# Query-key products of the prompt attention with 64-row operands instead of zero-padded 128-row operands

## The reference, cut to what matters

```python
logits = jnp.einsum('bqhmd,bkhmd->bhmqk', q, k).astype(jnp.float32) * (DA_DH ** -0.5)   # m = 0, 1; d = 64
bias = jnp.transpose(rel_bias[t5_bucket(dist)].astype(jnp.float32), (2, 0, 1))
logits = jnp.where((dist >= 0)[None, None, None], logits + bias[None, :, None], -1e30)
p = jax.nn.softmax(logits, axis=-1)
attn = p[:, :, 0] - lam * p[:, :, 1]
return jnp.einsum('bhqk,bkhv->bqhv', attn, v.astype(jnp.float32))
```

## Time and profile before

| | us |
|---|---|
| median of 3 runs | 1989.22 |
| lowest and highest run | 1988.94, 1991.32 |
| span of the profiled execution | 1994.6 |
| prompt attention | from 480.3 to some 912 |
| TensorE busy in the whole span | 1665.6 |
| VectorE busy | 730.8 |
| ScalarE busy | 454.2 |
| GpSimd busy | 266.4 |

### The profile page before, as it was taken

One profiled execution on the slowest core, in us unless ns is written; L12 is line 12 of the kernel. 1 busy time (PEld: TensorE's weight loads), 2 busy tenths in 40 slices (PEclk: granted clock), 3 DMA queues, 4 the chain that ended last, 5 costly groups with the idle time before them and its releaser, 6 DMA issues. The chain is left out here.

```text
span 1994.6 us, 22007 instructions
## 1 busy us (share of the span) xinstructions
PE 1665.6 (84%) x7402; PEld 1105.3 (55%) x7403; DVE 730.8 (37%) x1498; ACT 454.2 (23%) x1062; POOL 266.4 (13%) x479
## 2 busy tenths in 40 slices
PE   6998989775999999886996999999799059999950
PEld 4565556553555566553444888888587024444420
DVE  4267767674353535351223211121322312212213
ACT  2233332331343333331223111010322001111100
POOL 1001010101222222212130000000000311111112
PEclk8999989886999989997997999999899579999975
DMA  7001200002010100006764411210412838666426
GB/s 211 0 1 55 64 12 11 1 23 82 12 55 1 53 3 23 1 23 199 245 213 138 146 32 33 63 32 1 131 64 85 224 90 309 245 235 250 175 86 218
DMA packets 140800, 191.83 MB, mean 96 GB/s; under 512 B 10375, under 2 KB 107646, under 8 KB 140702
## 3 DMA queue, kind: packets, MB, share of 16 engines
q1 hardware_dynamic: 125022, 137.48, 22.1%
q0 software_dynamic: 15680, 53.10, 7.6%
HBM read 151.86 MB, written 38.69 MB: 96 GB/s over the span
## 5 line engine op out<-in xcount | busy, mean ns | idle before, releaser
L940 PE MATMUL psum<-branch_part,kept 128*128 128x384 f32 (+1 forms) x576 | 202.4, 507 | 1.2 <-DVE branch_part L1170 1.2
L2127 PE MATMUL psum<-moe_part,kept 128*128 x416 | 186.9, 603 | 5.6 <-DVE kept L2195 3.3
L940 PEld LDWEIGHTS psum<-branch_part,kept 128*128 128x128 f32 (+1 forms) x576 | 109.0, 194 | 77.0 <-issue 19.4
L1604 PE MATMUL psum<-split 128*128 128x368 f32 x384 | 133.3, 347 | 0.0
L474 PE MATMUL psum<-kept,branch_part 128*128 128x368 f32 x384 | 124.9, 481 | 10.0 <-PEq L217 5.0
L1598 PE MATMUL psum<-kept,merge_part 128*128 128x368 f32 x384 | 125.6, 481 | 9.0 <-DMA merge_part<-w_da_out 9.0
L2127 PEld LDWEIGHTS psum<-moe_part,kept 128*128 128x128 f32 x416 | 78.4, 193 | 95.9 <-issue 95.9
L479 PE MATMUL psum<-branch_part,kept 128*128 128x512 f32 (+1 forms) x288 | 127.5, 597 | 1.3 <-DVE kept L660 1.3
L1605 PE MATMUL psum<-split 128*128 128x368 f32 x384 | 126.8, 330 | 0.0
L1606 PE MATMUL psum<-split 128*128 128x368 f32 x384 | 126.4, 329 | 0.0
L1653 DVE TENSOR_TENSOR merge_part<-merge_part,psum 128x368 f32<-128x368 f32 x48 | 23.6, 534 | 254.0 <-ACT merge_part L1629 254.0
(11 more groups left out here) (307 smaller groups left out, 2713.2 us busy)
## 6 DMA issues: line engine op xcount, KB each, us to landing
branch_part<-cache_k SPq DMA_DIRECT2D x64, 256.0 KB, 4.9
branch_part<-cache_v POOLq DMA_DIRECT2D x64, 256.0 KB, 5.0
moe_part<-w_gate SPq DMA_DIRECT2D x16, 1024.0 KB
moe_part<-w_up SPq DMA_DIRECT2D x16, 1024.0 KB
moe_part<-w_down SPq DMA_DIRECT2D x16, 1024.0 KB
expert_out<-kept POOLq DMA_DIRECT2D x26, 512.0 KB, 4.1
branch_part<-w_in SPq DMA_DIRECT2D x8, 1024.0 KB, 8.8
merge_part<-w_in SPq DMA_DIRECT2D x16, 512.0 KB
```

What stands on the lines that cost most here:

```text
L940: mm = pe.matmul(bank_of(("z", h, i))[:ROWS[i], 0:384], K["xT"][:, k, cols(i)], Wb[h % 2][:, k, :], start=(k == 0), stop=(k == KC - 1))
L1604: pe.matmul(banks[j], wh[c % 2][:, k, ch], xh[:, k, chunk(n)], start=(k == 0), stop=False)
L2127: mm = pe.matmul(psum[:, 2 + par, :], XT[par][:, k, :], K["GU"][:, bass.ds(KC * b + k, 1), :], start=(k == 0), stop=(k == KC - 1))
```

## The change

The zero-padded tensors qz are replaced by one tensor qT that holds both maps, and each query-key product takes the 64 rows of its map from qT and from kT. The products of the two maps follow each other chunk by chunk (map 0 and map 1 of keys 0 to 511, then of the next chunk, then of the 16 meta keys), and not all of map 0 and then all of map 1. In tile 8 of a head the semaphore `logits` is raised after the last chunk of map 1 and no more after that of map 0. The 16 extra columns of tile 8 (job e) go to the same bank for both maps, and map 1's product now waits for map 0's through a new semaphore, `first_meta`. ScalarE places queries with one copy and not two, and for tile 0 of a head writes Qs itself with two more. GpSimd no longer clears qz and no longer copies into Qs. The tensor `vecs` shares memory with the probabilities. The rest of the kernel is as it was.

```diff
-            slot += [("L", s, 0), ("L", s, 1)] + ([("e", s, 0)] if s % NQ == NQ - 1 else [])
+            slot += [("L", s, 0)] + ([("e", s, 0)] if s % NQ == NQ - 1 else [])
...
-        qz = [sb(2, TOK) for _ in range(2)]
+        qT = [sb(TOK) for _ in range(2)]
...
-            def scores(s, m):
+            def scores(s):
+
                 h, i = s // NQ, s % NQ
                 r = P if i else META
-                q = qz[h % 2][:, m, COL[i]:COL[i] + r]
-                if m == 0:
-                    pe.wait_ge(x_done, NT * h + i + 1)
-                    if s:
-                        pe.wait_ge(exp_done, 2 * s)
+                half = [slice(0, 64), slice(64, P)]
+                pe.wait_ge(x_done, NT * h + i + 1)
+                if s:
+                    pe.wait_ge(exp_done, 2 * s)
                 n = P * i
-                for c in range(0, n, 512):
-                    w = min(512, n - c)
-                    mm = pe.matmul(lg[m][:r, c:c + w], q, kT[h % 2][:, FIRST + c:FIRST + c + w], start=True, stop=True)
-                if n < SEQ:
-                    mm = pe.matmul(lg[m][:r, n:n + META], q, kT[h % 2][:, 0:META], start=True, stop=True)
-                    mm.then_inc(logits, 1)
-                elif m == 0:
-                    mm.then_inc(logits, 1)
+                chunks = [(c, min(512, n - c), FIRST + c) for c in range(0, n, 512)] + [(n, META, 0)] * (n < SEQ)
+                for c, w, k0 in chunks:
+                    for m in range(2):
+                        mm = pe.matmul(lg[m][:r, c:c + w], qT[h % 2][half[m], COL[i]:COL[i] + r], kT[h % 2][half[m], k0:k0 + w], start=True, stop=True)
+                        if c == chunks[-1][0] and (n < SEQ or m == 1):
+                            mm.then_inc(logits, 1)
...
                 for m in range(2):
-                    mm = pe.matmul(bank_of(("e", s, 0))[:, META * m:META * m + META], qz[h % 2][:, m, cols(i)],
-                                   kT[h % 2][:, 0:META], start=True, stop=True)
-                mm.then_inc(logits, 1)
+                    rows = slice(64 * m, 64 * m + 64)
+                    if m:
+                        pe.wait_ge(first_meta, h + 1)
+                    mm = pe.matmul(bank_of(("e", s, 0))[:, META * m:META * m + META], qT[h % 2][rows, cols(i)],
+                                   kT[h % 2][rows, 0:META], start=True, stop=True)
+                    mm.then_inc(logits if m else first_meta, 1)
...
-                for m in range(2):
-                    rows = slice(64 * m, 64 * m + 64)
-                    act.activation(qz[h % 2][rows, m, cols(i)], bank[rows, 0:r], ACT.Copy, scale=K["vecT"][rows, 18:19])
+                act.activation(qT[h % 2][:, cols(i)], bank[:, 0:r], ACT.Copy, scale=K["vecT"][:, 18:19])
+                if i == 0:
+                    if h == 0:
+                        act.wait_ge(setup, 1)
+                    for m in range(2):
+                        rows = slice(64 * m, 64 * m + 64)
+                        act.activation(K["Qs"][rows, DB * h:DB * h + DB, 16 * h + 8 * m:16 * h + 8 * m + 8],
+                                       bank[rows, META:FIRST].rearrange("p (b s) -> p b s", s=DS), ACT.Copy, scale=K["vecT"][rows, 18:19])
...
-            for h in range(2):
-                pool.memset(qz[h].rearrange("p a b -> p (a b)"), 0.0).then_inc(setup, 1)
             pool.memset(K["Qs"].rearrange("p a b -> p (a b)"), 0.0).then_inc(setup, 1)
-            pool.wait_ge(setup, 3)
+            pool.wait_ge(setup, 1)
```

More of the change, by code:

```diff
@@ L850, in phase_attention @@
             "logits", "max_done", "exp_done", "a_done", "a_turned", "a_act", "a_dve", "o_done", "ssq_done", "orstd_done", "og_done", "og_turned", "ob_done"))
-        kv_out = [sem("kv_out0"), sem("kv_out1")]
+        kv_out, first_meta = [sem("kv_out0"), sem("kv_out1")], sem("first_meta")
         Wb = [sb(KC, 384) for _ in range(2)]
-        qz = [sb(2, TOK) for _ in range(2)]
+        qT = [sb(TOK) for _ in range(2)]
         kT = [sb(TOK) for _ in range(2)]
@@ L859, in phase_attention @@
         Bn = [sb(256) for _ in range(HEADS)]
-        rel, rel31, relh, bucket, vecs = sb(HEADS), sb(HEADS), sb(HEADS, P), sb(ND), sb(HEADS, ND)
+        rel, rel31, relh, bucket = sb(HEADS), sb(HEADS), sb(HEADS, P), sb(ND)
         Pm = sb(2, SEQ + META)
+        vecs = Pm.rearrange("p a b -> p (a b)")[:, 0:HEADS * ND].rearrange("p (a b) -> p a b", b=ND)
         Am, aT = sb(SEQ + META), sb(NT, P)
@@ L1012, in _ @@
                 pe.matmul(psum[:, h, 0:ND], relh[0:33, h, :], bucket[0:33], start=True, stop=True).then_inc(bias_made, 1)
-            run = {"z": product, "x": turn_qk, "L": scores, "e": lambda s, _: meta_scores(s), "a": turn_probabilities,
+            run = {"z": product, "x": turn_qk, "L": lambda s, _: scores(s), "e": lambda s, _: meta_scores(s), "a": turn_probabilities,
                    "o": lambda s, _: outputs(s), "g": lambda s, _: turn_output(s)}
@@ L1041, in place_qk @@
                 act.wait_ge(x_turned, n + 1)
-                if n == 0:
-                    act.wait_ge(setup, 3)
                 if i == 0 and h >= 2:
                     act.wait_ge(saved, h - 1)
-                for m in range(2):
-                    rows = slice(64 * m, 64 * m + 64)
-                    act.activation(qz[h % 2][rows, m, cols(i)], bank[rows, 0:r], ACT.Copy, scale=K["vecT"][rows, 18:19])
+                act.activation(qT[h % 2][:, cols(i)], bank[:, 0:r], ACT.Copy, scale=K["vecT"][:, 18:19])
[6 more added lines that the diff above has]
+                                       bank[rows, META:FIRST].rearrange("p (b s) -> p b s", s=DS), ACT.Copy, scale=K["vecT"][rows, 18:19])
                 act.activation(kT[h % 2][:, cols(i)], bank[:, P:P + r], ACT.Copy).then_inc(x_done, 1)
@@ L1136, in save @@
                 pool.wait_ge(x_done, NT * h + 1)
-                for m in range(2):
-                    pool.tensor_copy(K["Qs"][:, DB * h:DB * h + DB, 16 * h + 8 * m:16 * h + 8 * m + 8],
-                                     qz[h % 2][:, m, META:FIRST].rearrange("p (b s) -> p b s", s=DS))
                 pool.tensor_copy(K["kS"][:, h, :], kT[h % 2][:, 0:FIRST]).then_inc(saved, 1)
```

## The result

The changed kernel takes 2013.65 us (median of 4 runs, 2007.51 to 2018.51), the kernel before 1989.41 beside it. The ratio is 1.0118, with a 95% interval of 1.0081 to 1.0155: slower by some 24 us, where 3.5 were forecast, and outside the range of 1984 to 2002. The profiled execution has a span of 2011.9 us, 17.3 more than the one of before. Each run's time on record is its span and 1.9 us, so the profiled execution of before (span 1994.6) stands for a time of some 1996.5, 7 us above its median and not 5.4. That is why the two profiles differ by less than the medians do.

A forecast was written before the change was run, and what follows sets the result against it. The prediction took the chain through VectorE to bound the block: start -2.6, chain +1.0, clock +2.7 and +2.4 sum to +3.5 us, which on 1989.2 gives 1992.7 us. The range was 1984 to 2002.

The forecast's parts named there:

- What bounds the block: Prompt attention: each slot lasts as long as the chain through VectorE, and TensorE's saved time lengthens its own wait.
- Two row halves at work together: Query-key products: the two maps overlap on the row halves, so about 61 us of streaming become 31 us.
- Rival 1: Query-key products: no overlap on the row halves, map 0 ends later, about +32 us, 2021 us; chance 0.12.
- rival 2: Query-key products: both matmuls of map 0's 32-bit product precede map 1's, which lags; 4.4 us in all, 1997; chance 0.25.
- The terms of the chain: Slots of the prompt attention: shape changes +3.6 and +0.3 us, less waiting for map 1 and e -2.9, sum +1.0.
- The start: Start of the block: VectorE's table copy no longer held up by GpSimd's clearing, all behind it earlier, -2.6 us.
- The clock: TensorE falls to half clock after stretches with little work: +2.7 us and +2.4 us.
- the fourth head to lose its luck: Gap between heads, where the clock had held once: expected to fall there too, +3.3 x 0.8 = +2.7 us.
- one more such stretch and a little in the last slots: Short tiles: one more stretch at half clock, like head 0's loss of 1.7 us, and a little more, +2.4 us.

The follow-up runs named there:

- e2: Kernel before, its zero-padded 128-row products kept, but map 0 and map 1 of each chunk in turn: 2025.14 us, ratio 1.0181.
- k3: Changed kernel with the full fill of idle 128-row matmuls in TensorE's waits, repeated on another chip: 1980.64 us, ratio 0.9958.
- k4: Kernel before with idle matmuls in TensorE's waits and nothing else, repeated on another chip: 1982.17 us, ratio 0.9972.
- h3: Changed kernel with idle matmuls between heads alone (tiles 8 and 0): 2006.40 us, ratio 1.0081.
- g5: Changed kernel with 400 idle 128-row matmuls filling TensorE's waits for VectorE: 1977.28 us, ratio 0.9946.
- e3: Changed kernel with the matmuls of o done twice in tiles 0 to 6 of each head: 2000.26 us, ratio 1.0046.
- e1: Changed kernel with its 64-row products in the old order, all of map 0 and then all of map 1: 2006.15 us, ratio 1.0088.
- k1: Changed kernel with half as many idle matmuls as the full fill, of 128 rows: 1988.65 us, ratio 1.0004.
- k2: Changed kernel with half as many idle matmuls as the full fill, of 64 rows: 1990.96 us, ratio 1.0006.
- h1: Changed kernel with the full fill of idle matmuls, but of 64 rows: 1987.45 us, ratio 0.9982.
- g4: Kernel before with GpSimd's clearing of qz and the weights of head 1 issued later, and idle matmuls in TensorE's waits: 1976.94 us, ratio 0.9964.
- g3: Kernel before with GpSimd clearing qz later and the weights of head 1 issued later, without filling: 1985.77 us, ratio 1.0002.

## Why the prediction was wrong

**What bounds the block: right.** The chain through VectorE, and not TensorE's work. L to x in tile 7 is 5.65 us before and 5.54 after, with TensorE done 1.69 us before x; e2 delays map 0's logits alone, and each of its slots from tile 5 on grows by 1.0 to 1.3 us.

**Two row halves at work together: right.** The matmuls of a pair start 6 to 7 ns apart, and tile 7's twelve take 1.90 us, where before the first map alone took 1.67 and the last began 3.2 us after the first. Rival 1 is out, and rival 2 as well: the pairs are of map 0 and map 1, and in tile 7 VectorE didn't wait for map 1 behind map 0. Rival 1 was also priced too high: e2, which is that mechanism, shows some 19 us for it and not 28, since tiles 1 to 4 hide all of it.

**The terms of the chain: right in sign and size.** Map 0 starts 0.10 us later after L (0.2 forecast), map 1 gains 0.19 (0.19 forecast), and L to o in tile 8 gains 0.3 in each of the first three heads (0.42 less 0.2 forecast). The Trainium skill's rule that a change of tiling mode drains the engine (TensorEngine Tiling (Array Packing), Key Properties) fits that, at about 0.1 us on the way in. The whole chain term was +1.0 us. k3 and k4 bound it: with as much half clock in both, the two kernels differ by nothing in this stretch.

**The start: too high by 1.8 us.** The copy behaved as forecast (0.42 us). The block's start to the first z went from 11.35 to 10.57 us, 0.8 less and not 2.6: the weights land later than z could begin, as the text had allowed with "unless the weights of head 0 arrive later than the 488.9". The 0.55 us that it set beside the copy is a mean over four shapes; a copy of 512 from PSUM alone takes 0.68 in the kernel before. Nothing hangs on that.

**The clock: the step that failed.** The mechanism was named, and its term was far too small. The prediction put it at +2.7 us for "the fourth head to lose its luck" and +2.4 for "one more such stretch and a little in the last slots". It was ten more falls and 46 us more at half clock. The working treated the gap between heads as the place, and short tiles as an allowance. But the same text predicts waits of over 1.5 us in each tile 7. Behind such a wait is z, TensorE's longest piece of work, at 5.3 us; with the fall it takes 7.0. The earlier trace rows had the price, 7 matmuls in 3.4 us, and the mistake was to count one such place and not the slots in which the wait grows. h3 shows that the inner slots matter more. In the sum, the clock stood at +5.1 us, and 18 were measured between the two profiles.

The sum closes. With all but four of the falls gone the stretch takes 407.9 (g5) or 408.9 us (k3) in the changed kernel, and 408.9 (k4) in the kernel before. So the other falls cost before some 11.5 us and after some 29.5 to 30.5: 18 to 19 more, which covers the difference. That g5 and e3 shorten the kernel by adding nothing but work for TensorE shows the cause. For the median it is 24 us and not 18, because the profiled execution of before was one of its slower ones. The clocks of the runs agree: in whole executions the changed kernel's four runs have some 381 us at 1.2 GHz, by the estimate above, and the 14 of before that stand beside e1, on another chip, some 328. That is 54 us more for 24 us of time, where the profiles have 46 for 18.

What stays open: how much of it is the halved streaming and how much the 64 rows. The pair of places in k1 and k2 speaks for the rows; h1's profile and the equal times of k1 and k2 speak against a large part. e1 can't decide it, since its streaming is shorter and its waits are longer than before. Which version is best, g5 or g4, isn't told apart either: both are some 0.4 to 0.5% faster than before. The 64-row products earn nothing measurable once the waits are filled (0.9958 for k3 and 0.9972 for k4, with intervals that overlap).

## What to carry to other kernels

Before making an engine faster that waits for another one, ask what its clock does with the time saved: list every wait that grows, and what is queued behind it. Where TensorE waits a microsecond or more in each round of a loop, a few idle 128-row matmuls into a free bank are worth trying, first in the kernel as it is: here they gave 0.3% before the change and turned the change from 1.2% slower to 0.4 or 0.5% faster. Test the clock by adding work and not by removing it: a kernel that gets faster by it isn't bound by the work itself.

## What the runs showed of the hardware

- Two matmuls on different halves of the rows, 64 rows each, start 6 to 7 ns apart and stream together, with 32-bit operands too.
- The clock fell behind waits of under 2 us: TensorE was busy for 1.75 of 3.40 us, with a wait of 1.69 in it, and the next 3.4 us had a mean clock of 0.57.
- In two places the clock was held less well by few rows. At 2.67 us busy of 3.40 in both, it stayed with 128-row filling (k1) and fell with 64-row filling (k2). Also, the eight matmuls of 33 rows at the block's start were busy without a break (5.45 us) and stayed at 1.2 GHz: 5.45 / 8 = 0.68 us for 384 columns, where z's at full clock take 5.32 / 16 = 0.33. In the kernel before, z's matmuls of 128 rows followed at 491.66 us and had the full clock from 494.6 on. The Trainium skill (TensorE: Matmul & The Clock Gate, What's actually happening) describes the gate as watching how busy the engine is; the pair of k1 and k2 asks for the rows beside that.
- The copy of 512 numbers per partition on VectorE took 3.53 us beside GpSimd's clearing and 0.42 us without it, in the changed kernel and in g3, where the same clearings come later. The Trainium skill's exclusive lock on a pair of ports (SBUF — State Buffer, SBUF: two separate sides) would do just this.
- Filling TensorE before a wait cost nothing where the wait was longer than the filling: in k3 x still waited 0.35 us for VectorE in tile 7, and from L to x it was 5.54 us, as without filling.
